# Attention units on TensorE: transposes of the probabilities placed ahead of the scores

## What is computed

```
s = einsum('bqhgd,bqkhd->bqhgk', qg, ks) * (A_HEAD_DIM ** -0.5)
s = s - slopes * dist            # keys outside the chosen 256 (or 72) are pushed far away
p = softmax(s, axis=-1)
o = einsum('bqhgk,bqkhd->bqhgd', p, vs)
```

## Time and profile before

| | us |
|---|---|
| median of three runs | 2849.42 (2848.7 to 2849.43) |
| the profiled execution | 2844.89 |
| its span, first to last instruction | 2843.2 |
| TensorE busy in the span | 2691.2 (95%) |
| VectorE busy | 1344.7 (47%) |
| ScalarE busy | 695.2 (24%) |
| GpSimd busy | 467.3 (16%) |
| mean granted TensorE clock | 0.973 |

### The profile page before, as it was taken

The page is one execution under the profiler, slowest core; times in us unless marked ns, Lnnn a source line. Parts: engine busy times, 40 slices in busy tenths (PEclk is TensorE's granted clock), DMA queues, the critical chain, the costliest instruction groups (busy, mean ns, idle before and its releaser), DMA issues. The chain is left out here.

```text
span 2843.2 us, 41381 instructions
## 1 busy us (share of the span) xinstructions
PE 2691.2 (95%) x16384; PEld 2598.4 (91%) x16384; DVE 1344.7 (47%) x2834; ACT 695.2 (24%) x1162; POOL 467.3 (16%) x151
## 2 busy tenths in 40 slices
PE   8999999999987999999889997899999999999996
PEld 7999999999977889999888986898899999999995
DVE  3333333333343779999526673555533333333336
ACT  3111111111034444221525674001511111111102
POOL 1211111111111111222100000111121111111112
PEclk9999999999998999999989998999999999999998
DMA  4111111111012102232230001521111111111101
GB/s 151 45 44 44 44 44 44 44 44 44 17 38 69 28 23 53 92 95 58 75 116 2 9 1 46 194 72 39 45 45 44 44 44 44 44 44 44 44 15 61
DMA packets 144811, 149.11 MB, mean 52 GB/s; under 512 B 20240, under 2 KB 131440, under 8 KB 144576
## 3 DMA queue, kind: packets, MB, share of 16 engines
q1 hardware_dynamic: 141248, 134.45, 15.4%
q10 hardware_dynamic: 3456, 13.17, 1.1%
HBM read 123.82 MB, written 23.79 MB: 52 GB/s over the span
## 5 line engine op out<-in xcount | busy, mean ns | idle before, releaser
L477 DVE TENSOR_TENSOR ffn_prod<-ffn_gate,ffn_psu 128x384 f32<-128x384 f32 x132 | 69.5, 527 | 799.7 <-ACT ffn_gate L387 793.6
L67 PE MATMUL ixp_ps<-h_hi,ixp_hi 128*128 128x384 f32 (+1 forms) x1032 | 342.6, 332 | 35.7 <-ACT ix_stage L879 12.0
L387 ACT ACTIVATE ffn_gate<-ffn_psg 128x384 f32<-128x384 f32 x132 | 61.8, 468 | 1259.9 <-PE ffn_psu L69 1259.8
L67 PE MATMUL ffn_psd<-ffn_hid_hi,ffn_dn_hi 128*128 128x384 f32 (+1 forms) x1056 | 354.2, 335 | 12.7 <-DVE y L502 10.9
L67 PE MATMUL ffn_psg<-h_hi,ffn_up_hi 128*128 128x384 f32 (+1 forms) x1056 | 346.3, 328 | 8.4 <-DVE ffn_up_lo L402 6.6
L502 DVE TENSOR_TENSOR y<-y,ffn_psd 128x384 f32<-128x384 f32 (+1 forms) x480 | 251.0, 527 | 217.3 <-PE ffn_psd L69 217.3
L67 PE MATMUL ffn_psu<-h_hi,ffn_up_hi 128*128 128x384 f32 (+1 forms) x1056 | 344.0, 326 | 0.0
L69 PE MATMUL ffn_psd<-ffn_hid_hi,ffn_dn_lo 128*128 128x384 f32 (+1 forms) x1056 | 343.9, 326 | 0.0
L68 PE MATMUL ffn_psg<-h_lo,ffn_up_hi 128*128 128x384 f32 (+1 forms) x1056 | 343.8, 326 | 0.0
L68 PE MATMUL ffn_psd<-ffn_hid_lo,ffn_dn_hi 128*128 128x384 f32 (+1 forms) x1056 | 343.6, 325 | 0.0
L69 PE MATMUL ffn_psu<-h_hi,ffn_up_lo 128*128 128x384 f32 (+1 forms) x1056 | 343.0, 325 | 0.0
(11 more groups left out here) (303 smaller groups left out, 4919.7 us busy)
## 6 DMA issues: line engine op xcount, KB each, us to landing
ffn_dn_raw<-in_ffn_wd SPq DMA_DIRECT2D x22, 1024.0 KB, 4.9
ffn_up_raw<-in_ffn_wg SPq DMA_DIRECT2D x20, 1024.0 KB, 5.4
ffn_up_raw<-in_ffn_wu SPq DMA_DIRECT2D x20, 1024.0 KB, 7.9
ixp_raw<-in_w_in SPq DMA_DIRECT2D x39, 512.0 KB, 3.8
spill<-y ACTq DMA_DIRECT2D x15, 536.0 KB, 2.7
mo_sig<-spill SPq DMA_DIRECT2D x32, 192.0 KB, 4.1
spill<-ix_stage ACTq DMA_DIRECT2D x9, 536.0 KB, 2.7
y<-y_spill SPq DMA_DIRECT2D x1, 4288.0 KB, 14.1
```

The lines of the kernel that those rows point to most:

```text
L67: pe.matmul(out, w_hi, x_hi, start=first, stop=False)
L387: act.activation(self.gate[:, k % 2, 0:w], self.ps_gate[k % banks][:, 0:w], ACT.Silu).then_inc(self.silu_done, 1)
L477: dve.tensor_tensor(self.prod[:, k % 2, 0:w], self.gate[:, k % 2, 0:w], self.ps_up[k % banks][:, 0:w], ALU.mult).then_inc(self.prod_done, 1)
```

## The change

In the list of `pass_order`, T of unit n now stands ahead of S of unit n + 2 (and ahead of the Q that follows some S). V of unit n - 1 still follows both.

```diff
     for n in range(units + 1):
+        if n < units:
+            att.append(("T", n))
         if n + LOOK < units:
             att.append(("S", n + LOOK))
             if (n + LOOK) % HEADS == 3 and (n + LOOK) // HEADS + 1 < att_blocks:
                 att.append(("Q", (n + LOOK) // HEADS + 1))
-        if n < units:
-            att.append(("T", n))
         if n >= 1:
             att.append(("V", n - 1))
```

## The result

The change is slower: 2872.03 us as the median of 20 runs (2839.95 to 2877.06) against 2847.60 us for the kernel before (20 runs on the same chip, 2843.24 to 2851.73). The ratio is 1.0063, interval 1.0041 to 1.0085. It lies nearer to one than the ratio of the medians (1.0086), because it takes in every run, and some runs of the change were short. The profiled execution took 2873.77 us with a span of 2872.0 us, and its mean granted clock is 0.963 instead of 0.973.

A forecast was written before the change was run, and what follows sets the result against it. TensorE bounds the first half alone; in the second it waits for VectorE and ScalarE. Terms +1.8 +1.1 +0.7 -2.4 +0.5 -1.5 +0.9 gave +1.1 us on the 2849.42 median: 2850.5 us, range 2844.5 to 2857.

The forecast's parts named there:

- the first half: Mixers from 1480 to 1600 us, where TensorE has no idle time: the new order costs 0, bounds 0 and 1 us.
- Rival A: Units 52 to 64: ScalarE and VectorE late together and not paid back, +7.3 us, 2856.7 us; chance 0.19.
- The second half: Mixers from 1600 to 1760 us, where TensorE is idle 14.4 us: the part whose waits the change can move.
- Exponentials behind table loads: ScalarE's returns from square roots: T(52), T(58), T(64) wait 0.8, about 0.8, 0.65 us; V(51) starts 1.8 us later.
- X: T follows X at once and waits for its copy where nothing hides it, T(43) and T(75): 0.4 + 0.5 us.
- Stack of block 8: On ScalarE behind copies, table load and exponential: VectorE some 3.5 us late, S(61) waits about 1.8; V(59) 1.1 us later.
- V(63) and V(71): T ahead of S fills waits for VectorE behind these: -2.4 with 0.5 lost again at S(69), then -1.5 us.
- the three falls: TensorE's clock at 1.2 GHz behind waits of 0.92, 0.80 and 1.81 us, costing about 1.5, 1.5 and 3.7 us.
- rival B: Falls near 1705 us and behind the 1.81 us wait do not come: -4.1 us in all, 2845.3 us; chance 0.18.
- rival D: A table switch holds ScalarE beyond its load, so T(52), T(58), T(64) wait longer: +3.8, 2854.3 us; chance 0.01.
- My test for being wrong: Wrong if the first half grew over 1 us, T waited for exponentials in plain units, or clock falls were five-plus or none.

## Why the prediction was wrong

**The step that failed is the first: "For the first half I take 0, with bounds of 0 and 1 us".** It held for the work: in the whole change with wide scores, T(0) to T(40) takes 97.4 us, 1.2 more than before. Wider products are part of that, and so is the fall ahead of the stage, which lasted 2.5 us beyond T(0) there and 0.6 us before. It did not hold for the clock. I argued that an engine without idle time can gain or lose nothing by the order of its matmuls. The row that I read for this, 119.90 of 120 us busy at a clock of 0.98, says only that the clock had stayed up in that order. The change kept the engine as busy and lost 26.0 us, with the clock at 1.2 GHz for 61 us. The runs put in the place of that 0 a loss of about 26 us, all of it by the clock, that comes in most runs when units 8 to 15 have the new order and narrow products follow. All my falls of the clock stood behind waits of TensorE, so I looked for the clock only where the engine waits. Rival A, the only slower one with a real chance, looked in units 52 to 64 for the same reason.

**The second half came out as summed, by two errors that cancel.** The new order from unit 32 on gave 1.0007 times the time before. Of its terms:

- *Exponentials behind table loads.* T(52), T(58) and T(64) wait 0.74, 0.76 and 0.76 us; forecast 0.8, 0.8 and 0.65. Where no other fall came between, T(40) to T(56) grew by 1.2 us; forecast were +1.8 and 0.4 for X. Most of it is the stack of block 7 and not the exponential: with the stacks ahead again T(52) still waits 0.73 us, but T(51) waits 0.25 us for the output's copy instead of 1.06, and the stretch grew by 0.2 only. T(70) waits 0.53 where I had 0. Putting T(64) and T(70) back gained nothing.
- *Stack of block 8.* The place and the chain were right: S(61) waits 1.41 us (forecast 1.8), S(62) 1.63 in the change and 0.97 in the order from unit 32 on (forecast 1.0), VectorE waits 1.8 us for `mx_stack` (forecast 3). The size was not: T(56) to T(64) grew by 7.7 us, and I had 1.1 + 0.7. The stack moved ahead again takes 5.4 of it away, and with it the 13.7 us of low clock. I had written that "new ones appear (S(61), S(69))" of the waits and then gave them no fall. The mechanism is rival A's.
- *V(63) and V(71).* Both gains are there: S(68) does not wait, S(69) waits 1.15 us (forecast 1.5) and S(75)'s third piece 0.45 (forecast 0.6). T(64) to the end shrank by 7.8 us. My terms for that stretch in the sum (-2.4, +0.5, -1.5 and 0.5 for X) come to -2.9. I kept two of the three falls, and the -1.5 that I named for the first one never reached the sum. None came. That is rival B's mechanism, which I priced at -5.2 and gave 0.18.
- *X.* T(43) and T(75) wait 0.25 us each for the copy of X, forecast 0.4 and 0.5; and in the change the waits of 0.46, 0.69 and 0.74 us that T(51), T(59) and T(67) had for it are 0.25 each, which I had for the last alone.
- *The table load* (rival D): the exponential waits of T stayed at 0.53 to 0.76 us, and at T(58) the exponential starts 0.02 us behind its load (1669.09 + 1.28, next start 1670.39), so ScalarE lost nothing beyond the load. By the drain of about 1380 ns that the Trainium skill, page "ScalarE: Activation LUTs", section "What ACT_TABLE_LOAD costs", adds to a load, they would have been some 1.38 us longer, an estimate. The trace does not agree with that drain.

**My test for being wrong worked.** I wrote that the forecast fails "if the first half grew by more than 1 us", and that is the one that came. The other two signs did not come: behind T(0), T waited for exponentials only where a table load stood, and the stage had four falls of the clock, not five.

**What stays open.** Why the order of units 8 to 15 brings the fall is not settled. The width of the next block's products decides whether it comes; the number of narrow ones does not. But what TensorE does in the 272-key units is the same matmuls in either order, and no run tells which moment of it counts. Nor is it known why the same program takes the fall in 13 of 20 runs and not in the others. The group at 2853 us was never profiled. Its runs have a mean clock of 0.970, by the same estimate 41 us less at the lower level than the profiled run of the large group and 17 to 40 us more than the three shortest runs. One trace bears on it: where only units 16 to 23 were changed, the clock fell for 20.5 us at about 1650, in a part of the program that is word for word that of the kernel before, and that run took 2859.21 us. So a fall of that length can come without a change in the code around it, and such a fall in place of the long one could be what sets the middle group apart; that is argued and not shown.

## What to carry to other kernels

A TensorE that is busy all the time is not safe from an order: read the granted clock in small windows beside the busy share, and count matmuls per window. Where a stage of narrow products follows at the full clock, treat a new order ahead of it as a risk that the sum can't price, and give it a chance of its own. And price every new wait of TensorE with the fall that may follow: here one late stack, with its waits of 1.4 and 1 to 1.6 us and the fall behind them, cost 5.4 us, and its cure was to move a few instructions on another engine. The best version found applies the new order only where VectorE is late, from unit 62 on: 0.9975 of the time before, though its interval overlaps those of three other versions.

## What the runs showed of the hardware

- TensorE's clock can stand at 1.2 GHz for 61 us while the records show the engine busy all the time, with no idle gap ahead of it. A stretch of the recurrence's products shows what that costs one by one. After (line, shape, times, us busy, mean ns), from 1516 to 1577 us:

```profile
L1133 PE MATMUL mx_n<-rq,mx_state 128*128 128x80 f32 x32 | 10.5, 431 | 0.0
L1134 PE MATMUL mx_n<-mx_att,mx_rv_tok 80*128 80x80 f32 x32 | 10.1, 421 | 0.0
```

and before, in the same window:

```profile
L1134 PE MATMUL mx_n<-mx_att,mx_rv_tok 80*128 80x80 f32 x50 | 9.7, 275 | 0.0
L1133 PE MATMUL mx_n<-rq,mx_state 128*128 128x80 f32 x48 | 9.1, 271 | 0.0
```

- Whether a fall comes is not fixed by the program. The same kernel gave groups of runs some 10 and 20 us apart, each tight within itself, on one chip. A median of three could have landed in any of them.
- The length of a wait decides neither whether a fall follows nor how long it is. In the order from unit 62 on S(69) waited 1.15 us and no fall came, where before one came behind 0.80 us. And 3.4 us of low clock came with 2.03 us of T(58), 13.7 us with 1.43 us of S(61) and 0.97 us soon after.
